# Four edits to a fused three-layer kernel: first projections from raw weights, the entry of the mixing layer, the last down products, the order of the last gate

## What is computed

```python
h = gdn_mixer(x, ...)                     # layer 0: gated delta rule
x = layer_norm(ALPHA * x + h, ...)
x = layer_norm(ALPHA * x + swiglu(x), ...)
h = s5_mixer(x, ...)                      # layer 1: state space
x = layer_norm(ALPHA * x + h, ...)
x = layer_norm(ALPHA * x + moe_swiglu(x, ...), ln_g[1, 1], ln_b[1, 1])   # 8 experts, top 2
# layer 2
z = rmsnorm(x, g_mix) @ w_in              # b_gate, c_gate, x_in, u, v
x = x + concat(short_conv_mixer, sgu_mixer) @ w_out
x = x + hierarchical_moe(rmsnorm(x, g_ffn), ...)                         # 32 experts, top 2
gate = sigmoid(rmsnorm(x, g_ple) @ w_ple_gate)
x = x + gate * (p @ w_ple_proj)
return rmsnorm(x, g_final)

def layer_norm(x, g, b): return (x - mu) * rsqrt(var + LN_EPS) * g + b
```

## Time and profile before

| | us |
|---|---|
| median of 3 runs | 1507.8 |
| lowest and highest run | 1507.69, 1508.5 |
| the profiled execution | 1507.31 |
| its span in the profile | 1505.5 |
| PE busy | 1423.2 (95%) |
| DVE busy | 841.7 (56%) |
| ACT busy | 566.9 (38%) |

### The profile page before, as it was taken

One profiled execution on the slowest core, in us unless ns is written; L12 is line 12 of the kernel. 1 busy time (PEld: TensorE's weight loads), 2 busy tenths in 40 slices (PEclk: granted clock), 3 DMA queues, 4 the chain that ended last, 5 costly groups with the idle time before them and its releaser, 6 DMA issues.

```text
span 1505.5 us, 24226 instructions
## 1 busy us (share of the span) xinstructions
PE 1423.2 (95%) x10246; PEld 1001.3 (67%) x10246; DVE 841.7 (56%) x1358; ACT 566.9 (38%) x838; POOL 32.7 (2%) x32
## 2 busy tenths in 40 slices
PE   6999999999999999999899988999999999999987
PEld 6988879999988888873588437984443443443435
DVE  5777697899979679940589107772211212112127
ACT  5673337464443447730477003432111111110115
POOL 0000101000030000000000001000000000000001
PEclk9999999999999999999999999999999999999999
DMA  9441026454441239999999994599999999999991
GB/s 355 163 168 59 2 95 228 176 213 179 168 155 60 84 126 418 408 365 409 406 419 370 420 420 167 203 427 378 426 427 425 427 427 427 427 426 427 425 420 56
DMA packets 48354, 443.45 MB, mean 295 GB/s; under 512 B 6768, under 2 KB 7280, under 8 KB 17008
## 3 DMA queue, kind: packets, MB, share of 16 engines
q1 hardware_dynamic: 47088, 438.36, 71.7%
q10 hardware_dynamic: 1152, 3.46, 0.6%
HBM read 440.75 MB, written 1.05 MB: 293 GB/s over the span
## 4 chain that ended last, share of the span: by engine, by line
PE 74%; DVE 12%; DMA 8%; ACT 3%; issue 2%; PEldq 0%; DVEq 0%; ACTq 0%; PEld 0%; SPq 0%
PE psum L239 72%; DMA sb_spare<-moe_up 3%; DMA sb_work<-moe_up 3%; DVE sb_ring_r L1280 2%; DMA sb_ring<-moe_last 1%; DMA sb_work<-moe_last 1%; DVE sb_work L3040 1%; PE psum L2825 1%; DVE sb_ring_r L298 0%; PE psum L2230 0%; DVE sb_work L1374 0%; DVE sb_ring_r L524 0%; DVE sb_ring_r L2152 0%; DVE sb_work L1800 0%; DVE sb_work L1372 0%
## 5 line engine op out<-in xcount | busy, mean ns | idle before, releaser
L239 PE MATMUL psum<-sb_work 128*64 128x512 f32 (+13 forms) x3548 | 323.6, 342 | 23.5 <-DVE sb_work L3040 7.8
L239 PEld LDWEIGHTS psum<-sb_work 128*64 128x64 f32 (+5 forms) x3548 | 161.7, 143 | 160.7 <-issue 139.1
L239 PE MATMUL psum<-sb_ring,sb_work 128*64 128x512 f32 (+2 forms) x660 | 159.0, 599 | 12.7 <-DMA sb_ring<-moe_last 5.2
L239 PE MATMUL psum<-sb_xT_r,sb_ring_r 128*128 128x256 f32 x512 | 143.9, 283 | 0.0
L239 PE MATMUL psum<-sb_split 128*128 128x512 f32 (+1 forms) x398 | 128.7, 382 | 0.0
L239 PEld LDWEIGHTS psum<-sb_ring,sb_work 128*64 128x64 f32 (+1 forms) x660 | 51.5, 141 | 104.2 <-issue 98.1
L3038 DVE TENSOR_TENSOR sb_work<-sb_work,psum 128x512 f32<-128x512 f32 x16 | 11.0, 688 | 167.9 <-ACT sb_work L2950 167.9
L2950 ACT ACTIVATE sb_work<-psum 128x512 f32<-128x512 f32 x16 | 9.6, 598 | 240.2 <-PE psum L239 240.2
L239 PEld LDWEIGHTS psum<-sb_xT_r,sb_ring_r 128*128 128x128 f32 x512 | 98.2, 192 | 0.3
L3008 DVE SCALAR_TENSOR_TENSOR sb_out_even<-psum,sb_work,sb_out_even 128x512 fp32r<-128x512 f32 x32 | 22.6, 747 | 125.8 <-ACT sb_out_even L2936 125.8
L239 PE MATMUL psum<-sb_split,sb_lnp_r 128*128 128x512 f32 (+1 forms) x260 | 87.7, 376 | 4.1 <-DVE sb_ring_r L2152 3.7
(11 more groups left out here) (514 smaller groups left out, 2876.6 us busy)
## 6 DMA issues: line engine op xcount, KB each, us to landing
sb_work<-moe_up SPq DMA_DIRECT2D x33, 2048.0 KB, 25.8
sb_ring<-moe_wide SPq DMA_DIRECT2D x52, 1024.0 KB, 9.6
sb_ring<-w_dense SPq DMA_DIRECT2D x23, 2048.0 KB, 8.7
sb_work<-moe_wide SPq DMA_DIRECT2D x43, 1024.0 KB, 10.6
sb_ring<-moe_up SPq DMA_DIRECT2D x18, 2048.0 KB, 25.3
sb_work<-moe_down SPq DMA_DIRECT2D x17, 2048.0 KB, 24.0
sb_ring<-ffn_wide SPq DMA_DIRECT2D x14, 2048.0 KB, 7.5
sb_ring<-moe_down SPq DMA_DIRECT2D x9, 2048.0 KB, 25.2
```

What stands on the lines that cost most here:

```text
L239: return nc.tensor.matmul(o, lhsT, rhs, start=start, stop=stop, **kw)
```

## The change

1. **GDN start.** Pieces 0 and 1 (`PLAIN = 2`) are multiplied as fp32 from the loaded weights and x, without split, 8 matmuls for each. Ahead of them stand 16 fp32 fillers over a tile `warm` that POOL sets to 1. ACT and DVE split only piece 2 at first. All counts of the two semaphores fall by 2.
2. **Mixing entry.** ACT alone makes the centred, scaled rows `x_hat = (x - mean) * rstd` into `sb_spare`; PE turns these, without fillers ahead or between (14 stand behind). Gain and bias, multiplied by layer 2's gain by POOL far ahead (`ln_mix`), are applied on the way out of PSUM, chunks 0 to 3 by DVE (`hat_first`), 4 to 7 by ACT (`hat_second`). The normalised rows in `xres` are made by DVE only after the barrier, and `row_sums` of n = 4 come between the low parts of pieces 3, 4 and 5. ACT's roots of n = 4 move behind the high part of piece 6, PE's turn of them (`r_diag`) from behind piece 3 to behind piece 5.
3. **down_last.** Chunks 0 and 1 of both halves run when their loads are there, chunk 2 of both halves when its loads are there.
4. **PLE.** DVE makes the low part of the third gate piece ahead of the sums of half 0, that of the fourth between the halves; ACT makes one more high part ahead of the roots.

```diff
@@ row_moments @@
+            if n == 3:
+                ins = v.tensor_scalar(mean_neg[:, h, :], mv[:, h, 0:1], -1.0, None, ALU.mult)
@@ new functions @@
+        def hat_scalar(act, h):
+            norm_root(act, 3, h)
+            act.wait_ge(sem("rstd_ready"), 2 * 3 + h + 1)
+            act_link(act, act.activation(mean_off[:, h, :], mean_neg[:, h, :], ACT.Copy, scale=rstd[:, h, :]))
+            for q in range(2):
+                f = slice(512 * q, 512 * q + 512)
+                act.activation(x_hat[:, h, f], xres[:, h, f], ACT.Identity, scale=rstd[:, h, :], bias=mean_off[:, h, :])\
+                   .then_inc(sem("rows_normed"), 1)
+        def hat_first(v, h):
+            v.wait_ge(sem("turned"), 4 * TSTAGE[4] + 2 * h + 1)
+            for c, o, turned in hat_chunks(h, 0):
+                ins = v.tensor_scalar(o, turned, ln_mix[:, 0, c:c + 1], ln_mix[:, 1, c:c + 1], ALU.mult, ALU.add)
+            ins.then_inc(sem("mix2_operand"), 1)
+        def hat_second(act, h):
+            act.wait_ge(sem("turned"), 4 * TSTAGE[4] + 2 * h + 2)
+            for c, o, turned in hat_chunks(h, 1):
+                ins = act.activation(o, turned, ACT.Identity, scale=ln_mix[:, 0, c:c + 1], bias=ln_mix[:, 1, c:c + 1])
+            ins.then_inc(sem("xT_ready"), 2)
...
@@ gdn_tensor @@
-            for c in range(QKV):
+            pe.wait_ge(sem("zg_done"), 4)
+            for _ in range(16):
+                mm(bank[5][:, 0:P], warm, warm)
+            pe.wait_ge(sem("first_loaded"), 32)
+            for c in range(PLAIN):
+                pe.wait_ge(sem(f"piece_loaded{c}"), 16)
+                for k in range(DC):
+                    ins = mm(bank[c % 4][:, 0:SEQ], gd_piece(ring, c)[:, k, :], xT[:, k, :], k == 0, k == DC - 1)
+                ins.then_inc(sem("qkv_ps"), 1)
+            for c in range(PLAIN, QKV):
@@ down_last @@
-                for ab in range(2):
+                for ab, chunks in enumerate(((0, 1), (2,))):
                     for j in range(PACK):
                         half_loaded(pe, LAST_MEMBER, i + ab, j)
-                for n in range(2):
-                    for cc in range(FF_BLOCKS[2]):
+                    for n in range(2):
+                        for cc in chunks:
...
@@ mix2_tensor @@
-                if j == 0:
-                    pe.wait_ge(sem("mix2_operand"), HALVES)
+                    if (j, c) == (1, 1):
+                        pe.wait_ge(sem("mix2_operand"), 2 * HALVES)
@@ mix2_vector @@
-            for h in range(HALVES):
-                row_sums(v, 4, xres, h)
+            v.wait_ge(sem("rows_normed"), rows_at(3) + 4)
+            norm_half(v, 3, xres, xres, 0)
+            norm_half(v, 3, xres, xres, 1)
             dn_low(v, D_WIN2 + 3)
+            row_sums(v, 4, xres, 0)
+            dn_low(v, D_WIN2 + 4)
+            row_sums(v, 4, xres, 1)
+            dn_low(v, D_WIN2 + 5)
@@ ple_vector @@
-            row_sums(v, 6, xres, 0)
             v.wait_ge(sem("dense_low"), D_PLE + 2)
             dn_low(v, D_PLE + 2)
+            row_sums(v, 6, xres, 0)
+            dn_low(v, D_PLE + 3)
             row_sums(v, 6, xres, 1)
@@ tensor program @@
+                for h in range(HALVES):
+                    turn_half(pe, 4, x_hat, h)
                 awake(14, 0)
-                turn_half(pe, 4, xres, 0)
-                awake(6, 0)
-                turn_half(pe, 4, xres, 1)
-                pe.wait_ge(sem("xT_ready"), 4 * (TSTAGE[4] + 1) - 2)
-                awake(6, 0)
@@ scalar program @@
-                norm_scalar(act, 3)
-                x2_round(act, 4)
+                for h in range(HALVES):
+                    hat_scalar(act, h)
+                act.wait_ge(sem("s5_pool"), 6)
+                hat_second(act, 0)
+                hat_round(act, 0, 0)
+                hat_second(act, 1)
+                hat_round(act, 0, 1)
+                hat_round(act, 1, 0)
+                hat_round(act, 1, 1)
```

More of the change, by code:

```diff
@@ L552, in gd_split @@
         def gd_split(pe, s):
-            pe.wait_ge(sem("gdn_low"), 1 + s + 1)
+            pe.wait_ge(sem("gdn_low"), 1 + s - PLAIN + 1)
         GATES_AT = 8
+        warm = S[:, 0, :]
         SUMS_AT = (10, 14, 18, 22)
@@ L807, in gdn_scalar @@
             act.activation(gxh[:, :, :], xT[:, :, :], ACT.Copy).then_inc(sem("gdn_high"), 1)
-            for s in range(3):
+            for s in range(PLAIN, 3):
                 gd_high(act, s)
@@ L3557, in gate @@
                 act.activation(ple_g[i % 2], bank[4 + i][:, :], ACT.Sigmoid, scale=rstd[:, i % 2, :]).then_inc(sem("ple_sig"), 1)
-            for p in range(D_PLE + 4, D_END):
+            for p in range(D_PLE + 5, D_END):
                 dn_high(act, p)
@@ L3570, in ple_vector @@
         def ple_vector(v):
-            row_sums(v, 6, xres, 0)
             v.wait_ge(sem("dense_low"), D_PLE + 2)
             dn_low(v, D_PLE + 2)
+            row_sums(v, 6, xres, 0)
+            dn_low(v, D_PLE + 3)
             row_sums(v, 6, xres, 1)
-            for p in range(D_PLE + 3, D_END):
+            for p in range(D_PLE + 4, D_END):
                 dn_low(v, p)
@@ L3932, in layouts @@
     A["g_cols"] = np.stack([chunkcols(inp[n][0]) for n in ("g_mix_2", "g_ffn_2", "g_ple_2")], axis=1)
[L3933 removed]
+    A["ln_cols"] = np.stack([chunkcols(inp[n][1, j]) for j in range(2) for n in ("ln_g", "ln_b")], axis=1)
     A["conv2_w"] = inp["w_conv_2"][0].reshape(CONV2_TAPS, CW // P, P).transpose(2, 1, 0)
```

68 lines of the change are left out of this document (44 added, 24 removed).

## The result

| | median of the runs | profiled execution | its span |
|---|---|---|---|
| before | 1507.96 us (6 runs, 1507.69 to 1509.12) | 1507.31 us | 1505.5 us |
| after | 1498.36 us (6 runs, 1496.85 to 1500.29) | 1499.14 us | 1497.3 us |

The ratio is 0.9936, 95% interval 0.9923 to 0.9949: 9.6 us faster, where 7.4 were forecast. The two profiled executions differ by 8.2 us.

What follows compares the result with a forecast made beforehand. PE's chain was taken to bound the kernel, with MoE 2's DMA stream moving along. GDN 4.1, mixing entry net 2.6 (down products included) and PLE 0.7 sum to 7.4 us: 1500.4 us on the median's scale, range 1496.8 to 1505.0.

Steps and rivals of the forecast that it cites:

- the rival in which it absorbs the gains: DMA-paced MoE 2: its load stream does not move with PE, leaving only 0.7 us gain, 1507.1 us; chance 0.06.
- GDN start: First GDN products: piece 2 ends at 18.0 us instead of 22.14, gain 4.1 us (2.3 to 4.6).
- `down_last`: End of MoE 1: products following their loads hand 2.3 us to the mixing entry (1.5 to 2.6).
- entry itself: Mixing entry: first mixing product 3.5 us earlier, 2.3 of it from the down products.
- passes behind the barrier: Mixing stage: DVE's moved norm passes make low parts of pieces 3 to 5 late, cost 0.9 us (0 to 2).
- PLE: Gate products: low parts ahead of the sums remove two PE waits, gain 0.7 us (0.3 to 0.9).
- The cold start: Rival at GDN's start: PE falls to slow pace between fillers and piece 0, minus 1.8 us, 1502.2; chance 0.08.
- 32 transpose instructions: Mixing entry on PE: slow at first, half done at 915.9 us, all done at 918.0.
- The stall behind the branch: Rival at mixing entry: PE's pause follows the saturated loads' end, entry gives 0.8 us, total 4.8, 1503.0; chance 0.21.
- The pointer operands: ACT's entry operations: twelve would take some 1.1 us more, lowering the total gain by some 0.5 us.
- My turn of 3.3 against 2.9 us: Behind the mixing barrier: DVE's sums plus low part against PE's piece, pieces 4 and 5 each 0.4 us late.
- the two waits: PE's waits for low parts of gate pieces three and four: 0.58 us and about 0.15 us.

Runs made afterwards that it cites:

- e3: Kernel before with only the down_last part (chunks ordered by load); 1508.32 us, ratio 0.9989 to before.
- e7b: Changed kernel with 16 filler matmuls added on PE right behind the branch, ahead of the transposes; 1501.61 us, ratio 0.9959 to before.
- e9: Changed kernel with one plain GDN piece, low parts ahead of both row sums, and half 1's second scaling moved from ACT to DVE; 1496.69 us.
- e5b: Changed kernel without the 16 filler matmuls ahead of GDN's first products; 1498.16 us, ratio 0.9936 to before.
- e11: Changed kernel unaltered, measured again; 1496.66 us, ratio 0.9922 to before.
- e12: Kernel before with only the down_last part, unaltered repeat of that single-part run; 1506.65 us, ratio 0.9988 to before.
- e6b: Changed kernel without DVE's norm passes behind the mixing barrier (output wrong); 1497.12 us, ratio 0.9927 to before.
- e8b: Changed kernel with one plain GDN piece instead of two, and low parts of pieces 3 to 5 ahead of both row sums; 1497.93 us, ratio 0.9929.
- e10: Changed kernel with ACT's old order in the PLE stage, DVE's new order kept; 1496.86 us.

## Why the prediction was right, and where it was off

The direction was right, the range held the result (though the second measurement, 1496.66 us, lies 0.1 us below it), and so was the frame: PE's order sets the end, and MoE 2 moves whole. MoE 2 took 428.5 to 429.3 us in all 14 profiles, so the rival in which it absorbs the gains is refuted. The gain was under-sized in three terms, by the columns 10.7 us for 7.4.

| term | predicted | measured, means over the columns | |
|---|---|---|---|
| GDN start | 4.1 | 97.13 - 92.61 = 4.5 (4.2 in the first pair) | right, before's own profile was a short one |
| `down_last` | 2.3 | 328.50 - 325.54 = 3.0 (4 profiles against 10; 2.2 in the first pair) | top bound 2.6 passed |
| entry itself | 3.5 - 2.3 = 1.2 | 26.40 - 23.58 = 2.8 (2.4 in the first pair) | under-sized |
| passes behind the barrier | -0.9 | -0.85 | right |
| PLE | 0.7 | 1.25 | under-sized |
| sum | 7.4 | 10.7 | timed 9.6 and, again, 11.3 |

(GDN: the five profiles with the old start against the six with two plain pieces and fillers. The entry's means leave out e3 with its second pause, e7b and e9; with e3 the old entry's mean is 27.36.)

- **GDN** went as worked out: piece 0 at 7.93 us (8.0), copies at 15.11 and 17.94 (15.3 and 18.1). The cold start did not happen; e5b gives 1.5 us for it, near the 1.8 of that rival.
- **Entry.** The mechanism held, the size did not. The term that failed is "32 transpose instructions". I counted two for each, as a fp32 product has; the trace has 16, one each. From the end of the combine I had PE back after 6.5 us (it was 6.04), the transposes done 4.5 us later (it was 3.36), and the first product 3.4 us behind them (it was 3.73): 14.4 us in all, and it was 13.1. That 1.3 us is the whole error in the first pair (2.4 us for 1.2), most of it the transposes'; the 0.4 us more in the means is spread that no run explains. Which wait ends last was misnamed as well: in after it is ACT's rounding, 0.60 us behind PE's fillers; in e9, and nearly in e11, the fillers, as predicted.
- **The stall behind the branch** did not keep its place (e12), nor vanish (e7b). That it sets the start of the transposes, as I had it, holds in six of the eight kernels with the new entry and no added fillers: there the rows are ready 0.84 to 1.42 us before PE is. The new entry gains because the transposes follow the stall at once. In before, DVE's second pass over half 0 ended only at 918.40, 2.8 us behind the stall's end, and with 22 slow fillers between the transposes began at 920.08. With the old entry the stretch to the restart took 26.1 to 26.9 us in four profiles and 31.2 in the one with a second stop, with the new one 23.2 to 23.9 in eight; whether a second stop could happen there too is not shown. (In this rival's sum, 4.1 + 0.8 - 0.9 + 0.7 is 4.7 us, not 4.8.)
- **The pointer operands** that the Trainium skill (ScalarE: Activation LUTs, What ACT_TABLE_LOAD costs) prices at about 93 ns each: the trace agrees. Passes of 512 columns with two take 0.76 us, roundings without one 0.57; of 128 columns 0.375 with two, 0.278 with one. Against the 0.65 and 0.275 us that I had used, the twelve operations took 1.2 us more, near the 1.1 of that sentence, and the gain grew all the same.
- **The norm passes** came within 0.05 us. My turn of 3.3 against 2.9 us for a low part was the mechanism: PE's three late starts add up to 0.9 us, and e6b and e8b, without them, both bring back 70.56.
- **`down_last`.** That products follow the loads held, 0.69 us of wait left. Why 3.0 by the means and not 2.3 is not settled: the columns of both kinds of kernel vary by 2 to 3 us, the loads' times from issue to landing among them.
- **PLE.** "The chain behind is PE's" held; the two waits were mis-sized. I had read 0.58 us for the first from the bracket, which counts from a modelled end, and 0.15 for the second. By the starts of the products, 0.225 us apart where nothing waits, the third piece lost 0.83 us in before (1478.13, 1479.10, 1479.41) and the fourth 0.43, at
```profile
1482.21 0.19 PEld L239 LDWEIGHTS psum<-sb_ple_high,sb_xT_r 128*128 128x128 f32 x1 [0.57 <-DVE sb_ring_r L298]
```
That is 1.26 us, and the gain is 1.26. In after no start is late, and ACT's next-to-last high part, which waits for PE before and after, begins 11.29 us after the first gate product instead of 12.54. Behind it follow, as before, its last high part, the first gates and DVE's 11.2 us. e10 agrees: the third and fourth piece wait no more there, and 1.06 us are gained; its last 0.2 us are ACT's, whose high parts then stand behind the roots.

## What to carry to other kernels

Where an engine has a stop of its own, put the wait for another engine over it, and then ask which of the two ends last. The profile's bracket names only the semaphore (here the rows, which were ready 1.3 us earlier). Work that is moved behind a barrier is free if what others wait for (here the low parts) goes ahead of what nobody needs yet (the sums), and that order can be worked out as a rate, us a turn against us a piece. Size waits from start to start. Size small edits by fixed stretches of several profiles: the mixing and PLE stretches repeat to 0.05 us where the whole time of single runs differs by 4.
